# Experts written out: sums over three chunks in rotating visits, five row buffers, an earlier first split, the table's low product on ScalarE

## The reference, cut to what matters

```
def chunk(xc):
    q = (xc @ w_query).reshape(T, PEER_HEADS, 2, PEER_HALF)
    s = jnp.einsum('thpd,hpkd->thpk', q, sub_keys)
    ...                                   # two top_k levels give idx and top
    g = jax.nn.softmax(top, axis=-1)
    u = expert_down[idx]
    act = jax.nn.gelu(jnp.einsum('td,thkd->thk', xc, u), approximate=False)
    vv = expert_up[idx]
    return jnp.einsum('thk,thkd->td', g * act, vv)
...
x = x + gt2[:, None, :] * _peer(h2, ...)
return _rmsnorm(x, final_norm_g)
```

## Time and profile before

| | |
|---|---|
| runs | 3762.81, 3765.0, 3767.08 us; median 3765.0 |
| the profiled execution | 3768.69 us, of which the span is 3766.9 |
| mean granted clock of TensorE | 0.958 |
| PE busy | 3365.3 us (89%), 17315 matmuls |
| DVE busy | 2822.7 us (75%) |
| ACT busy | 959.2 us (25%) |
| POOL busy | 2126.8 us (56%) |
| HBM | 563.68 MB read, 93.88 MB written |

### The profile page before, as it was taken

The page is one execution under the profiler, slowest core; times in us unless marked ns, Lnnn a source line. Parts: engine busy times, 40 slices in busy tenths (PEclk is TensorE's granted clock), DMA queues, the critical chain, the costliest instruction groups (busy, mean ns, idle before and its releaser), DMA issues. The chain is left out here.

```text
span 3766.9 us, 54151 instructions
## 1 busy us (share of the span) xinstructions
PE 3365.3 (89%) x17315; PEld 2836.8 (75%) x17315; DVE 2822.7 (75%) x5260; ACT 959.2 (25%) x1545; POOL 2126.8 (56%) x1286
## 2 busy tenths in 40 slices
PE   3999978988798779999996999999999999999986
PEld 3888766776586668888886778878788777777864
DVE  5111056641479989999997888888988889888899
ACT  3111145431222223333332212121222212212211
POOL 3990000024133435555655777777877778777776
PEclk8999989999899989999998999999999999999997
DMA  4443110023221113444436788878888788888886
GB/s 182 131 123 106 62 46 12 12 90 134 78 67 55 51 59 113 157 164 160 152 134 226 256 258 265 278 248 274 264 265 278 244 270 256 273 255 266 268 259 222
DMA packets 405470, 660.35 MB, mean 175 GB/s; under 512 B 219648, under 2 KB 270920, under 8 KB 402640
## 3 DMA queue, kind: packets, MB, share of 16 engines
q1 hardware_dynamic: 324368, 364.01, 30.2%
q0 software_dynamic: 78656, 286.30, 22.4%
q10 hardware_dynamic: 2304, 8.39, 0.5%
HBM read 563.68 MB, written 93.88 MB: 175 GB/s over the span
## 5 line engine op out<-in xcount | busy, mean ns | idle before, releaser
L372 PE MATMUL psum<-e_u_hi,e_w_hi 128*128 128x512 f32 x1536 | 613.1, 399 | 102.1 <-DVE acc L2195 74.8
L373 PE MATMUL psum<-e_u_lo,e_w_hi 128*128 128x512 f32 x1536 | 607.4, 395 | 0.0
L374 PE MATMUL psum<-e_u_hi,e_w_lo 128*128 128x512 f32 x1536 | 605.8, 394 | 0.0
L2195 DVE TENSOR_TENSOR acc<-acc,psum 128x512 f32<-128x512 f32 x756 | 474.0, 676 | 3.9 <-PE psum L374 3.6
L2205 DVE SCALAR_TENSOR_TENSOR acc<-e_row,e_row_weights_staged,acc 128x1024 f32<-128x1024 f32 x256 | 389.0, 1520 | 94.3 <-DMA e_row<-in_expert_up,rows_of 88.8
L2200 DVE SCALAR_TENSOR_TENSOR e_row<-e_row,h_rows 128x1024 f32<-128x1024 f32 x256 | 361.6, 1422 | 111.1 <-DMA e_row<-in_expert_down,rows_of 109.7
L2319 POOL DMA_INDIRECT e_row<-in_expert_down,rows_of x256 | 342.7, 1339 | 161.9 <-DVE e_row L2200 118.4
L2319 POOL DMA_INDIRECT e_row<-in_expert_up,rows_of x256 | 348.8, 1362 | 149.0 <-DVE acc L2205 104.3
L372 PEld LDWEIGHTS psum<-e_u_hi,e_w_hi 128*128 128x128 f32 x1536 | 294.0, 191 | 182.5 <-DVE acc L2195 75.3
L1852 POOL TENSOR_TENSOR g_hot<-g_hot,g_lo 128x512 fp32r<-128x512 bf16 x192 | 230.7, 1202 | 256.5 <-DVE g_hot L1820 256.5
L2330 POOL TENSOR_TENSOR e_u_lo<-e_up,e_u_hi 128x1024 fp32r<-128x1024 f32 x128 | 368.0, 2875 | 1.3
(11 more groups left out here) (267 smaller groups left out, 7817.9 us busy)
## 6 DMA issues: line engine op xcount, KB each, us to landing
e_up<-in_expert_up SPq DMA_DIRECT2D x128, 512.0 KB
gate_table<-g_table SPq DMA_DIRECT2D x12, 4096.0 KB, 12.4
e_table<-gate_table SPq DMA_DIRECT2D x128, 384.0 KB
e_left<-in_expert_downT SPq DMA_DIRECT2D x60, 512.0 KB
e_left<-gelus_ahead SPq DMA_DIRECT2D x68, 384.0 KB, 5.3
ga_downT<-in_expert_downT SPq DMA_DIRECT2D x48, 512.0 KB, 4.3
gelus_ahead<-ga_gelu SPq DMA_DIRECT2D x48, 384.0 KB
pw_raw<-in_w_in SPq DMA_DIRECT2D x34, 512.0 KB, 3.8
```

What stands on the lines that cost most here:

```text
L372: nc.tensor.matmul(out, l_hi(k), r_hi(k), start=k == 0, stop=False)
L373: nc.tensor.matmul(out, l_hi(k), r_lo(k), start=False, stop=False)
L374: mm = nc.tensor.matmul(out, l_lo(k), r_hi(k), start=False, stop=k == steps - 1)
L2195: nc.vector.tensor_tensor(out, out, m.psum[:, 2 + x % BANKS], ALU.add).then_inc(acc_d, 1)
```

## The change

1. Table stage: the low product moves from GpSimd to ScalarE, as four ACTIVATEs of 128x128 with the token's low gate as a scale pointer, issued two groups ahead (`LEAD`). GpSimd keeps only `rest`. The stage also loads and splits one block more, the first that `experts` needs (`t.first_hi`, `t.first_lo`).
2. `experts` is written out, chunk by chunk, with no loops. `up(n)` takes 4 of the 12 groups (`VISITS`) over the three chunks before it (`SPAN`), the groups rotating; 130 rounds. W and U keep four buffers, freed by the new semaphore `freed`.
3. Five row buffers; the fifth lies where `gate2` was, which is stored to DRAM at the start and loaded again at the end. The slots are spread by shares: 4 for a fresh chunk, 1 for a ready one, the tail included.
4. Orders: ScalarE makes `U_hi` before the gelus and before `W_hi`; GpSimd in a fresh chunk `U_lo`, four fetches, `W_lo`, the other fetches, in a ready one `W_lo`, `U_lo`, fetches. SP asks for the down block of the next fresh chunk ahead of that chunk's table plane and up block. VectorE adds four groups a chunk. The order of the tiles at the end is 6, 7, 2, 3, 4, 5, 0, 1.

```
@@ gate_table
+    t.first_hi, t.first_lo = ah.hi[:, STEPS % 2], ah.lo[STEPS % 2]
+    LEAD = 2
...
         def _(pool):
             ah.rest(pool, 0, 0)
-            pool.wait_ge(lo, 1)
-            pool.wait_ge(rows_made, 2 * GTILES)
...
-                    nc.gpsimd.tensor_tensor(hot[y % DEEP][:, 2], hot1[y % DEEP][:],
...
-                    if y == GS - 1 and not last(n):
-                        ah.rest(pool, n + 1, 1 - u)
+                ah.rest(pool, n + 1, 1 - u)
...
+            def low(g, y):
...
+                act.wait_ge(hot1_d, g + 1)
+                at_least(act, done, g - (DEEP - 1))
+                for c in range(GT):
+                    made = nc.scalar.activation(hot[y % DEEP][:, 2, c], hot1[y % DEEP][:, c], ACT.Copy,
+                                                scale=cols(g_lo[:].bitcast(F32), g * GT + c, 1))
+                made.then_inc(hotlo_d, 1)
...
-                if not last(n):
-                    ah.split(act, n + 1, 1 - u)
+                ah.split(act, n + 1, 1 - u)
                 for y in range(GS):
                     g = n * GS + y
+                    low(g + LEAD, (y + LEAD) % DEEP)
                     act.wait_ge(done, g + 1)
@@ experts
-    PER = GROUPS // 2
-    BANKS = PER
-    RING = 4
+    SPAN = 3
+    VISITS = GROUPS // SPAN
+    WRING = SPAN + 1
+    BANKS = 6
+    RING = 5
...
+    share = [4 if is_fresh(c) else 1 for c in range(NG)]
+    first_slot = [2 * SLOTS * sum(share[:c]) // sum(share) for c in range(NG + 1)]
...
+    def visits(n):
+
+        return [(VISITS * (n - 1) + i, (VISITS * (n - 1) + i) % GROUPS) for i in range(VISITS)]
+
+    def chunks_of(n):
+        return range(max(n - SPAN, 0), min(n, NG))
...
+            sp.dma_start(t.gate2_dram, t.gate2[:]).then_inc(kept, 16)
+            load_up(0)
+            for buf in range(2):
+                sp.wait_ge(t.table_stored[buf], 16 * SD // TABLE_TOKENS // 2)
+            load_table(0)
+            load_down(1)
+            load_gelu(1)
+            for c in range(1, NG):
+                load_table(c)
+                load_up(c)
+                if c + 1 < NG and not is_fresh(c + 1):
+                    load_gelu(c + 1)
+                elif c + 1 < NG and fresh_no(c + 1) + 1 < FRESH:
+                    load_down(fresh_no(c + 1) + 1)
...
+            def up(n):
+                mine = chunks_of(n)
+                for J, j in visits(n):
+                    at_least(pe, acc_d, J - BANKS + 1)
...
+                    for c in mine:
+                        if c == n - 1 and J == visits(n)[0][0]:
+                            pe.wait_ge(w_lo, c + 1)
+                            pe.wait_ge(u_lo, c + 1)
...
+                if is_fresh(c):
+                    f = fresh_no(c)
+                    up_high(c)
                     for h in range(NH):
                         act.wait_ge(a_done, f * 2 + (h + 1))
...
+                    weight_high(c)
+                    if f + 1 < FRESH:
+                        downT(f + 1)
+                else:
+                    up_high(c)
+                    weight_high(c)
...
+            for c in range(NG):
+                mine = list(slots(c))
+                if is_fresh(c):
+                    for s in mine[0:4]:
+                        slot(s)
+                    landed(c)
+                    gate(c, 0)
+                    for s in mine[4:5]:
+                        slot(s)
+                    gate(c, 1)
+                    for s in mine[5:]:
+                        slot(s)
...
+                        for J, j in visits(c):
+                            add(J, j)
+                else:
+                    landed(c)
+                    gate(c, 0)
+                    gate(c, 1)
+                    if is_fresh(c + 1):
+                        downT(fresh_no(c + 1))
...
+                    for x, (J, j) in enumerate(visits(c)):
+                        add(J, j)
+                        if x < len(mine):
+                            slot(mine[x])
...
+                mine = [s + RING for s in slots(c)]
+                if is_fresh(c):
+                    rest_u(c)
+                    for s in mine[0:4]:
+                        fetch(s)
+                    rest_w(c)
+                    for s in mine[4:]:
+                        fetch(s)
+                else:
+                    rest_w(c)
+                    rest_u(c)
+                    for s in mine:
+                        fetch(s)
```

More of the change, by code:

```diff
@@ L1868, in _ @@
             nc.scalar.activation(g_hi[:], rT[:, 2], ACT.Copy).then_inc(hi, 1)
+            def low(g, y):
+                if isinstance(g, int) and g >= STEPS * GS:
+                    return
+                act.wait_ge(hot1_d, g + 1)
[4 more added lines that the diff above has]
+                made.then_inc(hotlo_d, 1)
+            act.wait_ge(rows_made, 2 * GTILES)
+            act.wait_ge(lo, 1)
+            for g in range(LEAD):
+                low(g, g)
             def step(n, q):
@@ L1891, in step @@
                 u, buf = q % 2, q // BS
-                if not (isinstance(n, int) and n >= STEPS - 2):
+                if not last(n):
                     ah.load(sp, n + 2, u)
@@ L2108, in up_part @@
                     rows = slice((j // 2) * P, (j // 2 + 1) * P)
                     cols = slice((j % 2) * HALF, (j % 2 + 1) * HALF)
-                    three_pass(nc, m.psum[:, 2 + x % BANKS], lambda k: W_hi[:, pair + k, rows],
-                               lambda k: W_lo[:, pair + k, rows], lambda k: U_hi[:, pair + k, cols],
-                               lambda k: U_lo[:, pair + k, cols], 2).then_inc(b_grp, 1)
-            def step(g, f, e, q, down, w):
-                if is_fresh(g, q):
-                    activations(f)
-                if not (isinstance(g, int) and g < 2):
-                    up_part(g, q)
@@ L2119, in _ @@
-            every(pe, step)
-            up_part(NG, 0)
-            up_part(NG + 1, 1)
+                    to = m.psum[:, 2 + J % BANKS]
+                    for c in mine:
+                        if c == n - 1 and J == visits(n)[0][0]:
+                            pe.wait_ge(w_lo, c + 1)
+                            pe.wait_ge(u_lo, c + 1)
+                        q = c % WRING
+                        nc.tensor.matmul(to, W_hi[:, q, rows], U_hi[:, q, cols], start=c == mine[0], stop=False)
+                        nc.tensor.matmul(to, W_hi[:, q, rows], U_lo[:, q, cols], start=False, stop=False)
+                        mm = nc.tensor.matmul(to, W_lo[:, q, rows], U_hi[:, q, cols], start=False, stop=c == mine[-1])
+                        if c == n - SPAN and c < NG - WRING and J == visits(n)[-1][0]:
+                            mm.then_inc(freed, 1)
@@ L2123, in _ @@
+                    mm.then_inc(b_grp, 1)
+            for c in range(NG):
+                if is_fresh(c):
+                    activations(fresh_no(c))
+                if c:
+                    up(c)
+            for n in range(NG, LAST + 1):
+                up(n)
         @block.scalar
```

390 lines of the change are left out of this document (152 added, 238 removed).

## The result

The changed kernel takes 3681.9 us (median of four; three lie between 3677.6 and 3684.5 with a median of 3679.4, the fourth, at 7015, is a disturbed execution and is left out of the ratio), the kernel before 3763.9 beside it: a ratio of 0.9777 (0.9758 to 0.9796). Forecast were 3626, a range of 3605 to 3650 for the forecast itself and one of 3580 to 3695 with the rivals. The sign and the wide range held, the narrow one did not; of the 139 us forecast, 82 came (84 by the median of the three).

A forecast was written before the change was run, and what follows sets the result against it. Bounds taken: VectorE stalled by GpSimd in the table stage, a fetch-slot-add loop in the pairs. Gains 35 table, 12 join, 59 pairs, 33 tail sum to 139: 3765-139 = 3626 us; own range 3605 to 3650, with rivals 3580 to 3695.

The forecast's parts named there:

- Table stage: Low product on ScalarE ends TensorE's wait for GpSimd's subtraction: step 12.8 to 12.0 us, gain 35, bounds 10 and 38.
- rival 5: Pairs: the PSUM wait becomes one for W_lo behind four fetches; pairs stay at 26.2, 3673 us; chance 0.08.
- rival 2: Pairs: the SP loop keeps the old period or slightly more, 26.4 to 27.1 us; 3685 to 3726; chance 0.13.
- rival 4: Table stage gives nothing: product is 1.53 by itself or ScalarE needs over 12.0 a step; 3661 us; chance 0.08.
- Join: Between table and expert stages: first down block split earlier, second block split about 2052; gain 12, bounds 5 and 16.
- Plane landed 2043 (384 KB take 5.3): Join: first table plane, asked for at 2038.12 behind the last table store, lands 5.3 us later.
- Pairs: Expert stage: 59 fresh-and-ready chunk pairs go from 26.4 to 25.4 us; gain 59, bounds gain 95 and loss 41.
- the loop through SP: Pairs: up load behind down load, which waits for VectorE's subtraction; 25.7 us with seven slots, 24.05 with six.
- 11.9+x+y: SP loop's length with seven slots; x, three loads issued and landed, 7.8; y, a row's landing, 6.0.
- a cover of 4 us: Pairs: slack between W_lo of the fresh chunk being ready (12.5 or later) and TensorE wanting it (16.5).
- the loop of the fetches: Pairs: loop of row fetches behind the ready chunk, 24 us with four adds and unstalled gates.
- Tail: After the experts' last activations: fewer slots a chunk bring 120 us to 87; gain 33, bounds 20 and 38.

The follow-up runs named there:

- e3: Changed kernel with the table's low product back on GpSimd instead of ScalarE: 3708.7 us.
- e11: Kernel of e1; at the first chunk row fetches wait for the plane, gates precede slots, gelus precede U_hi, W_lo follows two fetches: 3604.7 us.
- e1: Changed kernel with SP asking for the next down block behind the fresh chunk's table plane and up block, not ahead: 3600.4 us.
- e2: Changed kernel with GpSimd's four row fetches ahead of U_lo and W_lo in a fresh chunk: 3688.0 us.
- e6: Kernel before, with each expert-stage add after the first chunks covering 320 of 512 columns: 3761.2 us.
- e9: Kernel before, with down and gelu loads behind table plane and up block on SP, and adds on 320 of 512 columns: 3729.6 us.
- e5: Changed kernel with four row buffers instead of five: 3749.3 us.
- e8: Kernel of e1; at the first chunk down and gelu loads wait for the plane, gates precede the fifth slot, W_lo follows two fetches: 3600.3 us.

## Why the prediction was right or wrong

*The sum.* It held by the wide range. 3681.9 lies outside the forecast's own 3605 to 3650, nearer to rival 5's 3673 and rival 2's 3685 than to 3626. Of the 89.3 us between the two profiles 74.2 came from the table stage and the tail, where 68 were forecast; the join and the pairs gave 15.3 of 71. That the verdict held in spite of the pairs, the largest part, is owed to a range that took in rivals with other causes.

*Table stage: right.* 35 forecast, 36.9 in the two profiles, some 32 by all traces, and 27 by e3's time. Rows for its steps: a low product of ScalarE, all of TensorE's waits for the subtraction in the stage, and VectorE's product (lines; timeline):

```profile
L1867 ACT ACTIVATE g_hot<-g_hot,g_lo 128x128 fp32r<-128x128 bf16 x763 | 242.5, 393 | 0.0
```
```profile
L1282 PE MATMUL psum<-hT_hi,ga_downT_hi 128*128 128x512 f32 (+1 forms) x762 | 268.6, 352 | 2.4 <-POOL ga_downT_lo L1274 2.4
```
```profile
1719.54 0.68 DVE L1835 TENSOR_TENSOR g_hot<-g_hot,g_hi 128x512 fp32r<-128x512 bf16 x1
```

A step is 12.0 us. The product went from 1.53 to 0.68, so 1.53 was never its own length (rival 4).

The Trainium skill (SBUF — State Buffer, SBUF: two separate sides) says that VectorE and GpSimd hold their shared port for a whole instruction; these rows agree.

The ACTIVATE came at the upper price, 393 ns by the 401 of the earlier trace rows, and ScalarE's 420.9 of 576 us left room for it. The subtraction at a step's head still stretches one `is_equal`, to 2.9 us, but TensorE no longer waits for it.

*Join: wrong, 12 forecast and 2.6 got.* The idle time ahead of the first activations fell to 4.3, as said. The step that failed is "Plane landed 2043 (384 KB take 5.3)". SP's requests and TensorE's second wait in the changed kernel:

```profile
1988.10 0.43 SPq L1904 DMA_DIRECT2D gate_table<-g_table  x1
...
2001.28 0.68 SPq L2061 DMA_DIRECT2D e_table<-gate_table  x1
...
2018.07 0.80 PE L2118 MATMUL psum<-e_u_hi,e_w_hi 128*128 128x512 f32 x1 [15.92 <-POOL e_w_lo L2335]
```

The price was the median of gelu blocks of the same size; the page of the profile has none for a plane. This plane had the rows' 2 MB, the up block and gate2's copy in front of it, all asked for from 1991 on beside the 4 MB store, and took some 12 (VectorE's gate started at 2013.08); e11 gave 5.5 where the rows weren't in front. The prediction had seen this queue (335 GB/s, 93% busy) and charged it only with 1.6 us for gate2's copy. So where about 10 us of waiting ahead of up(1) were forecast, 15.9 came. A second term was small too: up(1) was put at 2.7 us and took 5.3 (2018.07 to 2023.36), its matmuls 0.43 us apart instead of 0.23, as TensorE starts at the lower of its two clocks after the wait (0.80 for the first matmul; granted share 0.70 in this stretch).

*Pairs: the loop right, its size wrong, 59 forecast and 12.7 got.* That the loop through SP would be the bound, that ScalarE's wait for the up block would show it, and that TensorE would no longer wait for adds, all came true, with e1 as the proof. The steps that failed are terms of 11.9+x+y. Here are their means over the 54 loops of 2100 to 3500, from the end of one subtraction to the end of the next (timelines of VectorE, ScalarE and GpSimd):

| term | forecast | measured |
|---|---|---|
| x, to the start of U_hi | 7.8 | 9.0 |
| U_hi, U_lo, hand-offs | 4.25 | 3.9 |
| from U_lo to the last slot (fetch and y) | 7.1 | 6.9 |
| the slot | 1.28 | 1.8 |
| adds, gates, subtraction | 4.75 | 4.6 |
| sum | 25.1 (25.4 with TensorE's floor) | 26.2 |

So x was put 1.2 us too low (the highest forecast was 8.7) and the slot 0.55, and the other terms held within 0.4. The sum measured is the pair.

TensorE's side had a term at nothing. Four fetches and W_lo (7.1+1.9 in the pair above) stand between U_lo and TensorE's product and end even with the row's landing; the prediction gave W_lo a cover of 4 us. TensorE's wait for it in mid-pair is one of the signs by which the prediction said that it would be wrong, and it came: 59.7 us, 1.1 a pair. Rival 5 named this wait and its price, 26.2 a pair, and both were met. Its cause was not: e2 takes the fetches from between U_lo and W_lo and changes nothing, e1 leaves them there and ends the wait.

The slots of the pairs grew because GpSimd's subtractions now run beside more of them (the 5.63 above, beside 1.86 and 2.41 on GpSimd), to the means below from 1415 and 1453 ns before. In the traces of both kernels a slot beside which no subtraction runs takes 1.25 us in the mean and 1.29 at most; a subtraction runs beside 131 of 424 slots before (1.84 us in the mean) and beside 212 of 446 after (2.41):

```profile
L2221 DVE SCALAR_TENSOR_TENSOR acc<-e_row,e_row_weights,acc 128x1024 f32<-128x1024 f32 x221 | 402.1, 1819 | 69.6 <-DMA e_row<-in_expert_up,rows_of 61.3 <-DVE acc L2221 0.5
L2212 DVE SCALAR_TENSOR_TENSOR e_row<-e_row,h_rows 128x1024 f32<-128x1024 f32 x225 | 396.3, 1784 | 69.9 <-DMA e_row<-in_expert_down,rows_of 69.5
L2206 DVE TENSOR_TENSOR acc<-acc,psum 128x512 f32<-128x512 f32 x428 | 271.2, 676 | 0.0
```

Eight slots times 0.37 are 3 us a pair, more than the 2.4 that the fewer adds saved: VectorE is busy 23.5 us of a pair (1253.9/1400 of 26.20) where it was 22.9.

Not borne out was a step ahead of that sum: the loop of the fetches was brought down to 24 in part by "four adds" for six. In the kernel before, e6 and e9 take as much off the adds and put it at nothing. What pays in this part is the fifth buffer (67 us in the changed kernel, e5), which the prediction named beside the adds and gave no price of its own.

*Tail: right*, 33 forecast, 37.3 got, up parts of 8.2 us with three gaps of under 1 between them.

*Left open:* why the changed kernel with four buffers takes 0.75 a pair more than the kernel before. Longer slots (1575 and 1630 ns there) would fit; no run separates them from the new places of slots and fetches. The kernel before with five buffers wasn't tried. The sums over three chunks and the writing out of the loops, forecast at nothing by itself, weren't undone alone, so no run gives their worth.

## What to carry to other kernels

When loads share one issuing queue, ask of each what it must wait for, and put those whose buffers are free first: one load that waits for the engine at the end of the loop makes all behind it part of the loop (82 us here, for two moved lines). Price a saving on the engine that waits by what it waits for: in the kernel before, 2.4 us a pair off VectorE's adds gave nothing while it waited for rows, and in the changed one a row buffer more gave 67 us. Price a transfer at a stage's border by what is queued in front of it, not by its median in mid-stage.

## What the runs showed of the hardware

- A plane of 384 KB landed in 5.5 us (e11), or in 11.2 to 11.8 with some 2 MB of row fetches asked for ahead of it; 0.9 MB asked for behind it made 0.5 us at most (11.2 in e8 against 11.7 in e1).
- An fp32 add from PSUM took 211 ns for 64 columns, 307 for 160, 342 for 192, 476 for 320 and 677 for 512: some 1.04 ns a column on 141 to 145 ns. Adds that follow each other start 0.598 us apart with 512 columns and 0.132 with 64, some 0.08 less than they last.
- A ScalarE copy of 128x128 with a scale pointer took 393 ns, against 255 without one from PSUM.
- A slot of 1.28 us took 5.63 beside two GpSimd subtractions that followed each other without a gap, while the adds, which read one operand from PSUM, kept their 676 ns: 425 of 636 before and 147 of 428 after ran beside such a subtraction, and none took over 0.69 us. In e1 the slots were longer still (1846 and 1901 ns) and the pairs shorter, since VectorE's 23.2 us (1315.6/1400 of 24.7) still fit under TensorE's 24.7.
